# The short convolution of the first mixer moved from VectorE to GpSimd

## The reference

```python
def short_conv_mixer(b_gate, c_gate, u, conv_w):      # each 256 tokens x 512 channels
    v = c_gate * u
    vp = jnp.pad(v, ((0, 0), (2, 0), (0, 0)))
    conv = vp[:, 0:S] * conv_w[0]
    for j in range(1, 3):
        conv = conv + vp[:, j:j + S] * conv_w[j]
    return b_gate * conv

z = h @ w_in
b_gate, c_gate, u, q, k, v = jnp.split(z, [c1, c2, c3, c4, c5], axis=-1)
ya = short_conv_mixer(b_gate, c_gate, u, conv_w)
yb = sliding_window_attention(q, k, v, sinks, table)
return jnp.concatenate([ya, yb], axis=-1) @ w_out
```

## Time and profile before

| | us |
|---|---|
| median of 3 runs | 1610.01 (1609.54 to 1612.07) |
| the profiled execution: its own time | 1612.29 |
| the profiled execution: its span | 1610.6 |
| PE busy in it | 1573.1 (98%) |
| DVE busy | 1129.3 (70%) |
| ACT busy | 831.7 (52%) |
| POOL busy | 80.0 (5%) |

### The profile page before, as it was taken

How to read it: one execution, slowest core, us unless ns; L and a number is a source line. 1 busy time by engine, 2 the same in 40 slices (tenths; PEclk the granted TensorE clock), 3 DMA queues, 4 the chain that set the end, 5 groups by cost and what they waited for, 6 DMA issues and landing times.

```text
span 1610.6 us, 23784 instructions
## 1 busy us (share of the span) xinstructions
PE 1573.1 (98%) x9061; PEld 1370.5 (85%) x9061; DVE 1129.3 (70%) x1605; ACT 831.7 (52%) x1164; POOL 80.0 (5%) x139
## 2 busy tenths in 40 slices
PE   7999999999999999999999999999999999999997
PEld 6788899888888888889988888878888998788885
DVE  6776668667667676675766867677666796776666
ACT  5554555555555555455555555455544641554454
POOL 0400002000000000000002800000000000000000
PEclk9999999999999999999999999999999999999999
DMA  7756553545555565554434565646555451465551
GB/s 259 244 180 208 183 182 128 184 136 181 184 195 171 169 222 173 197 185 159 148 131 131 185 221 171 205 151 209 197 194 170 127 181 34 138 209 208 182 185 51
DMA packets 208528, 280.60 MB, mean 174 GB/s; under 512 B 5183, under 2 KB 183785, under 8 KB 208457
## 3 DMA queue, kind: packets, MB, share of 16 engines
q1 hardware_dynamic: 206080, 274.50, 51.1%
q0 software_dynamic: 1360, 3.80, 0.8%
q10 hardware_dynamic: 1016, 1.32, 0.3%
HBM read 278.55 MB, written 2.63 MB: 175 GB/s over the span
## 4 chain that ended last, share of the span: by engine, by line
PE 87%; DVE 7%; ACT 3%; issue 1%; DMA 1%; DVEq 0%; ACTq 0%
PE bank L1559 37%; PE bank L1610 29%; PE bank L1609 13%; DVE w_lo L947 3%; PE bank L1612 2%; PE bank L2041 2%; ACT w_hi L522 1%; PE bank L1666 1%; PE bank L1819 1%; PE bank L1790 1%; ACT xT L550 1%; PE bank L1808 0%; DVE xT L987 0%; DMA raw<-in_xa_w_q 0%; PE bank L1711 0%
## 5 line engine op out<-in xcount | busy, mean ns | idle before, releaser
L947 DVE TENSOR_TENSOR w_lo<-raw,w_hi 128x1024 fp32r<-128x1024 f32 x514 | 616.2, 1228 | 228.0 <-ACT w_hi L522 227.0
L1610 PE MATMUL bank<-xT,w_hi 128*128 128x512 f32 x2112 | 737.5, 398 | 5.1 <-DVE arena L1059 3.4
L522 ACT ACTIVATE w_hi<-raw 128x1024 fp32r<-128x1024 f32 x514 | 527.0, 1051 | 147.8 <-PE bank L1610 83.7
L1609 PE MATMUL bank<-xT,w_lo 128*128 128x256 f32 x1848 | 516.8, 280 | 0.6 <-DVE w_lo L1216 0.6
L1610 PEld LDWEIGHTS bank<-xT,w_hi 128*128 128x128 f32 x2112 | 383.9, 188 | 81.7 <-DVE arena L1059 4.0
L1609 PEld LDWEIGHTS bank<-xT,w_lo 128*128 128x128 f32 x1848 | 349.4, 189 | 13.6 <-DVE w_lo L1216 0.9
L1559 PE MATMUL bank<-w_hi,hid_hi 128*128 128x512 f32 x528 | 208.6, 395 | 2.9 <-DVE w_lo L947 2.9
L1559 PE MATMUL bank<-w_lo,hid_hi 128*128 128x512 f32 x528 | 206.6, 391 | 0.0
L1559 PE MATMUL bank<-w_hi,hid_lo 128*128 128x512 f32 x528 | 206.6, 391 | 0.0
L1559 PE MATMUL bank<-xT,w_hi 128*128 128x256 f32 x800 | 146.6, 285 | 1.9 <-DVE w_lo L947 1.1
L1559 PEld LDWEIGHTS bank<-xT,w_hi 128*128 128x128 f32 x800 | 124.6, 191 | 4.9 <-issue 3.1
(11 more groups left out here) (263 smaller groups left out, 1641.4 us busy)
## 6 DMA issues: line engine op xcount, KB each, us to landing
raw<-in_ffn_w_down SPq DMA_DIRECT2D x44, 1024.0 KB, 5.5
raw<-in_ffn_w_in SPq DMA_DIRECT2D x44, 1024.0 KB, 5.1
raw<-in_ffn_w_gate SPq DMA_DIRECT2D x43, 1024.0 KB, 5.4
raw<-in_ffn_w_up SPq DMA_DIRECT2D x43, 1024.0 KB, 5.4
raw<-in_ffn_w_out SPq DMA_DIRECT2D x22, 1024.0 KB, 5.3
raw<-in_w_in SPq DMA_DIRECT2D x10, 1024.0 KB, 5.3
raw<-in_xa_w_kv SPq DMA_DIRECT2D x8, 1024.0 KB, 5.8
raw<-in_od_w_in SPq DMA_DIRECT2D x8, 1024.0 KB, 5.4
```

What stands on the lines that cost most here:

```text
L522: act.activation(hi, src, ACT.Copy).then_inc(sem["hi_ready"], 1)
L947: dve.tensor_tensor(lo, src, hi.bitcast(F32), ALU.subtract).then_inc(sem["lo_ready"], 1)
L1609: pe.matmul(bank[:, b, T:2 * T], lo, xT_hi[:, k, :], start=False, stop=False)
L1610: last = pe.matmul(bank[:, b, :], hi, xT[:, k, :, :], start=k == 0, stop=k == KD - 1)
```

## The change

POOL's program now has everything of the short convolution: the zeros of the pad, the six scalings, the two products, the taps and the gates. A tap is a multiplication by a coefficient that is broadcast along the tokens, over both groups of 128 channels at once; for the second and third tap an addition follows. That is five instructions of 128x512 elements for each half, each waiting for the end of the one before through the new semaphore `conv_step`. DVE's program loses the same work, and keeps everything else in the same order. ACT's, PE's and SP's programs are the same.

```diff
             pool.wait_ge(sem["scale_ready"], 2)
-            for n, m in enumerate((conv_c[:, 0, :], conv_u, conv_c[:, 1, :], conv_u, conv_b[:, 0, :], conv_b[:, 1, :])):
-                pool.wait_ge(sem["nat_sb"], (1, 2, 4, 5, 6, 7)[n])
-                m = m.rearrange("p (s t) -> p s t", s=2)
-                pool.tensor_tensor(m, m, scale_row[:, None, :].to_broadcast([P, 2, T]), ALU.mult)\
-                    .then_inc(sem["scaled"], 1)
...
+            def step(ins):
+
+                nonlocal steps
+                steps += 1
+                ins.then_inc(sem["conv_step"], 1)
+                pool.wait_ge(sem["conv_step"], steps)
+
+            def scale(m, ready):
+
+                pool.wait_ge(sem["nat_sb"], ready)
+                step(pool.tensor_tensor(pairs(m), pairs(m), scale_row[:, None, :].to_broadcast([P, 2, T]), ALU.mult))
+
+            for n in range(2):
+                step(pool.memset(conv_v[:, n, 0:2], 0.0))
+            w = COL_OF["conv_w"]
+            for n in range(2):
+                scale(conv_c[:, n, :], 1 + 3 * n)
+                scale(conv_u, 2 + 3 * n)
+                pool.tensor_tensor(conv_v[:, :, 2:2 + T], pairs(conv_c[:, n, :]), pairs(conv_u), ALU.mult)\
+                    .then_inc(sem["conv_v_ready"], 1)
+                pool.wait_ge(sem["conv_v_ready"], n + 1)
+                y, product = pairs(conv_y[:, n, :]), pairs(conv_c[:, n, :])
+                for j in range(3):
+                    at = w + 4 * j + 2 * n
+                    tap = cols[:, at:at + 2][:, :, None].to_broadcast([P, 2, T])
+                    step(pool.tensor_tensor(product if j else y, conv_v[:, :, j:j + T], tap, ALU.mult))
+                    if j:
+                        step(pool.tensor_tensor(y, y, product, ALU.add))
+            for n in range(2):
+                scale(conv_b[:, n, :], 6 + n)
+                pool.tensor_tensor(conv_y[:, n, :], conv_y[:, n, :], conv_b[:, n, :], ALU.mult)\
+                    .then_inc(sem["conv_ready"], 1)
...
-            for n in range(2):
-                link(dve.memset(conv_v[:, n, 0:2], 0.0))
...
             dve.wait_ge(sem["half_done"], v + 9)
             dve.tensor_tensor(swa_k, bank[:, 4, 0:T], scale_row[:, :], ALU.mult).then_inc(sem["proj_sb"], 1)
-            conv_product(0)
             split()
-            conv_taps(0)
...
             splits(2)
-            conv_product(1)
-            conv_taps(1)
-            for n in range(2):
-                dve.wait_ge(sem["scaled"], 5 + n)
-                dve.tensor_tensor(conv_y[:, n, :], conv_y[:, n, :], conv_b[:, n, :], ALU.mult)\
-                    .then_inc(sem["conv_ready"], 1)
             split()
```

More of the change, by code:

```diff
@@ L300, in build @@
             q_ready proj_sb nat_sb scores max_ready exp_ready probs_ready probT_psum probT_even probT_odd
-            out_psum y_hi_ready y_lo_ready conv_v_ready conv_ready conv_tap dve_step act_step
+            out_psum y_hi_ready y_lo_ready conv_v_ready conv_step conv_ready conv_tap dve_step act_step
             rank_psum decays gla_operands gla_scores score_ready kv_psum states_ready ln_ready
@@ L453, in _, with pairs @@
             pool.wait_ge(sem["scale_ready"], 2)
-            for n, m in enumerate((conv_c[:, 0, :], conv_u, conv_c[:, 1, :], conv_u, conv_b[:, 0, :], conv_b[:, 1, :])):
-                pool.wait_ge(sem["nat_sb"], (1, 2, 4, 5, 6, 7)[n])
-                m = m.rearrange("p (s t) -> p s t", s=2)
-                pool.tensor_tensor(m, m, scale_row[:, None, :].to_broadcast([P, 2, T]), ALU.mult)\
-                    .then_inc(sem["scaled"], 1)
+            def pairs(m):
+                return m.rearrange("p (s t) -> p s t", s=2)
+            steps = 0
+            def step(ins):
[26 more added lines that the diff above has]
+                    .then_inc(sem["conv_ready"], 1)
             pool.wait_ge(sem["max_ready"], 6)
@@ L1411, in _ @@
                 dve.wait_ge(sem["nat_sb"], NAT_BEFORE_2 + 2 + 2 * n)
-                dve.wait_ge(sem["scaled"], 6 + n + 1)
+                dve.wait_ge(sem["scaled"], n + 1)
                 s = slice(2 * n, 2 * n + 2)
```

## The result

| | before, us | changed, us |
|---|---|---|
| median of 10 runs | 1609.95 (1608.80 to 1612.11) | 1614.70 (1613.53 to 1615.93) |
| span of the profiled execution | 1610.6 | 1613.5 |
| POOL busy | 80.0 | 98.0 |
| DVE busy | 1129.3 | 1132.1 |

The ratio is 1.0026, 95% interval 1.0016 to 1.0036: the changed kernel is slower by about 4.2 to 4.8 us, with 2.6 and 5.8 as bounds. The forecast was 1617.5 with a range of 1611 to 1621.5; the direction and the mechanism were right, the size was 7.5 instead of 4.75.

The account below looks back on a forecast made before the run. PE, 98% busy, was taken as the bound. Output projection 8.75 us late, less 2.00 us idle time, plus 0.7 for the clock, made +7.45: 1610.0 + 7.5 = 1617.5 us, range 1611 to 1621.5 (8 in 10).

Parts of the forecast that it names:

- The bound: PE bounds the kernel; taking the second half's convolution off DVE regains at most 2.00 us idle and 1.4 us clock.
- The first half: Convolution work before the logits: already hidden, so no gain; DVE's tiny instructions wait 0.25 to 1.4 us, taken as 0.8.
- The second half: Ten POOL instructions beside DVE's 13 contending ones in the softmax: normalisation ends at 279.6 us instead of 269.25.
- Turns: POOL and DVE alternate on SBUF, each waiting for the other's whole instruction; likeliest case, chance 0.52, 1615 to 1620 us.
- pairs: Rival in the softmax: DVE's splits and probability scalings pass two at a time between POOL instructions; +3.7, 1613.7 us, chance 0.22.
- On the path: PE's last transposes come 8.05 us late, the output projection 8.75; less 2.00 us idle time at the mixer's end, +6.75.
- the copies: DVE's three copies (L1189, 0.69 us each) queue behind the normalisation; the last ends some 0.7 us later after the transposes.
- the clock of the stall: PE's idle time of some 7 us at 271 us lowers its clock afterwards, costing 1.4 to 2.8 us.
- Normalising free: Rival: the probability scaling doesn't contend with POOL, only tiny additions and splits wait; about -1, 1609 us, chance 0.08.
- POOL slower: Rival: broadcast coefficients or shifted starts cost POOL more than 1.28 us an instruction; +11, 1621 us, chance 0.10.
- Faster: Rival: DVE wins nearly every turn, POOL's convolution moves after 269.25 us; gain 2.00 + 1.4, 1606.6 us, chance 0.08.

Follow-up runs that it names:

- e6: Kernel before, with the two splits that free the last weight unit's slot put ahead of the second half's convolution on VectorE and ScalarE: 1607.97 us, ratio 0.9993.
- e8: Kernel before, with VectorE adding the first part of the residual ahead of the mixer's last two splits, not after them: 1607.49 us, ratio 0.9986.
- e2: Changed kernel with only the first half's product and taps on GpSimd; second half's product and taps and both gates back on VectorE: 1610.03 us, ratio 1.0000.
- e3: Changed kernel with the first half's product and taps back on VectorE; second half's and both gates on GpSimd: 1614.06 us, ratio 1.0031.
- e4: Changed kernel with four redundant 128x512 multiplications added on GpSimd in the second half, between first and second tap: 1614.27 us, ratio 1.0036.
- e7: Changed kernel with the second half's five tap instructions replaced by five GpSimd memsets of 128x1024, which only write: 1611.16 us (one run).
- e10: Changed kernel with the probabilities of groups 2 to 5 scaled by one two-input 128x512 VectorE instruction instead of two of 128x256: 1615.15 us, ratio 1.0029.
- e1: Changed kernel with GpSimd's second-half product waiting until VectorE has normalised all six softmax groups: 1613.80 us, ratio 1.0027.
- e5: e1 with the DMA that reloads the bias table issued ahead of GpSimd's second half instead of behind the gates: 1610.96 us, ratio 1.0005.
- e9: The edits of e5 and e8 together: second half on GpSimd after the normalisation, reload first, residual ahead of two splits: 1607.24 us, ratio 0.9984.

## Why the prediction was right

**The bound.** Right as an upper bound. e6 and e8 get most of PE's 2.00 us and the clock's dip back without GpSimd, some 1.8 and 2.2 us in the medians where 3.4 had been reckoned. In e8's trace the product behind the next norm starts at 301.19 us instead of 305.73, which is 3.1 us earlier when the 1.4 us that this trace lies ahead from the start are taken off; that the medians show only 2.2 stays open.

**The first half.** Nothing gained and one turn lost: forecast 0.8 us, measured 0.74 (0.90 for 0.16). e2 shows it to be free.

**The second half.** Turns, one VectorE instruction for one of GpSimd: right, with "pairs" wrong nearly throughout. That the one-input scaling takes part was inferred from the earlier trace rows, which is weak ground (two instructions lost 0.27 us together, not a turn of 0.396 each); the 1.5 to 2.6 us of L1213 show it. Forecast for the end of the normalisation was 279.6, or 278.6 by this trace's offset; measured 277.02, 1.6 us less. This is the term that was mis-sized: the three multiplications of the taps took 1.04 us each and not 1.28, 0.7 us together, and a tiny addition slipped through without a turn, so that VectorE was done 0.4 us behind GpSimd's last instruction and not 1.3. The claim behind the sum that each GpSimd instruction costs a turn holds only up to saturation; here supply and demand happened to be about equal, at ten, and in so far it was luck that the sum came out near.

**On the path.** By the offset, PE comes to the last transposes at 277.07 instead of 270.55: 6.5 us late, against 8.05 forecast. The 0.7 us for the copies and the clock of the stall (1.4 to 2.8) came to 2.7 us together: from the last transposes to the output projection it is 5.9 us (277.07 to 282.97), where it was 3.2 before. PE resumed behind the mixer's last wait at 302.55 against 296.10, 7.45 us later by the offset; the forecast had 8.85 there, 6.75 and some 2.1 for the stall's clock. The dip at 297 us that is gone gave 1.4 back, so that the mixer costs 5.96 us: the same product behind the next norm starts at 310.67 instead of 305.73 in the chains of the two. Forecast 7.45.

**From 5.96 to 4.75.** Behind the mixer the distance of the two traces stays at 4.8 to 4.9 us until PE's idle time of 2.89 us at 1085 to 1092 us, which both kernels have. Before, it is followed by a stretch at the lower clock; in the changed kernel it is not. PE by time in the kernel before and one of its stretches, then both of the changed kernel:

```profile
1087.66 0.47 PE L1559 MATMUL bank<-w_hi,hid_hi 128*128 128x512 f32 x1 [2.89 <-DVE w_lo L947]
...
1284.43 0.39 PE L1559 MATMUL bank<-xT,w_hi 128*128 128x256 f32 x1 [0.82 <-DVE w_lo L947]
```

```profile
1088.50:1092.00 3.50, 3.50 (x10) 2.76 (x9) 3.50 (x5) 1.07 (x2) 0.00 (x0) 0.52 0.56 166
```

```profile
1092.44 0.47 PE L1565 MATMUL bank<-w_hi,hid_hi 128*128 128x512 f32 x1 [2.89 <-DVE w_lo L979]
...
1287.61 0.39 PE L1565 MATMUL bank<-xT,w_hi 128*128 128x256 f32 x1 [0.81 <-DVE w_lo L979]
```

```profile
1093.00:1096.50 3.50, 3.50 (x17) 2.92 (x16) 3.50 (x5) 1.36 (x2) 0.00 (x0) 1.00 0.41 146
```

The distance falls from 4.78 to 3.18 us, 1.6 given back. That leaves 5.96 less 1.6, or 4.4 us, and the medians differ by 4.75; executions of one kernel lie 2 to 3 us apart, so the rest can't be placed. No part of the forecast had this term. It isn't chance of one trace: the profiles of e3, e4, e7 and e10, which have the stall in the softmax, show full clock behind that idle time too, and those of e1, e2, e5, e6, e8 and e9, which haven't, show the dip. The time alone doesn't sort them: in e1 PE resumes at 1089.47 with the dip, in e7 at 1088.44 without. Why a stall at 270 us should decide over the clock at 1090 was not tested, and stays open.

**The rivals.** "Pairs" gave 1613.7, a number nearer to the median than the forecast's, by a mechanism that the trace refutes. "Normalising free" is refuted by L1213's 1.5 to 2.6 us, "POOL slower" by 1.04 to 1.31 us an instruction. "Faster" would have needed VectorE to win its turns; e1 and e5 made that so by a wait, and got back only to where the kernel before was, since the turns were then taken with the splits behind.

## What to carry to other kernels

Work moved from VectorE to GpSimd still holds VectorE up where it runs beside VectorE's contending instructions: in this kernel each GpSimd instruction of 1.0 to 1.3 us made one VectorE instruction wait for it. So count as moved only the work that falls beside VectorE's PSUM reads, reductions or idle time. Before moving it, look for what PE's wait truly hangs on; here one change of VectorE's order won 2.2 us, and the offload tried on top of it added nothing that can be measured. And when a step in an engine's order is made later, what stands behind it moves too: a reload of 1 MB cost 2.8 us by landing beside the wrong weight unit.

## What was not expected of the hardware

A GpSimd multiplication of 128x512 with one input broadcast along the elements took 1.04 us, with the two inputs dense, or one of them a row of 256 used twice, 1.26 to 1.31. A GpSimd memset, which reads nothing, left two-input VectorE instructions alone and stretched the one-input scaling from 0.62 to 1.78 us for two, as theory B of e7 had it. A reload on GpSimd's queue beside a weight unit on SP's made the unit take 8.16 us instead of 5.6 to 5.7.
